# Low parts, evictions, copies and table loads moved within the heads, and the norm factors formed in folded shape at the stage edges

## What is computed

```python
for i in range(DEPTH):
    h = rms_norm(x, W['norm_mix'][i])
    mixed = (hgrn2_mixer, diff_attn_mixer, rwkv7_mixer)[i % 3](h, ...)
    x = x + mixed
    x = x + swiglu(rms_norm(x, W['norm_ffn'][i]), W['ffn_w_in'][i], W['ffn_w_out'][i])
y = rms_norm(x, W['final_norm'])
```

## Time and profile before

| | |
|---|---|
| median of 3 runs | 3368.26 us (3367.20 to 3368.73) |
| the profiled execution, its own time | 3362.62 us |
| its span in the trace | 3361.0 us |
| PE busy | 3209.1 us (95%) |
| DVE busy | 1832.5 us (55%) |
| ACT busy | 1080.8 us (32%) |
| POOL busy | 131.4 us (4%) |
| mean granted PE clock | 0.985 |

### The profile page before, as it was taken

The page is one execution under the profiler, slowest core; times in us unless marked ns, Lnnn a source line. Parts: engine busy times, 40 slices in busy tenths (PEclk is TensorE's granted clock), DMA queues, the critical chain, the costliest instruction groups (busy, mean ns, idle before and its releaser), DMA issues.

```text
span 3361.0 us, 82189 instructions
## 1 busy us (share of the span) xinstructions
PE 3209.1 (95%) x35272; PEld 3041.2 (90%) x35272; DVE 1832.5 (55%) x3017; ACT 1080.8 (32%) x1754; POOL 131.4 (4%) x247
## 2 busy tenths in 40 slices
PE   8998999999998999997999999899999999899998
PEld 7887899998787999996988888899999888799998
DVE  6666643445655543437367887543344666654343
ACT  3222321223555321222434443332223222332221
POOL 0000000001322000000000000000000000000000
PEclk9999999999999999998999999899999999999999
DMA  3322222223433332221210000222232222223222
GB/s 124 102 83 65 85 89 88 86 98 96 129 119 97 87 95 81 88 93 61 82 34 19 12 20 15 61 88 92 83 97 78 84 89 83 71 83 96 81 91 77
DMA packets 104598, 269.08 MB, mean 80 GB/s; under 512 B 12802, under 2 KB 45954, under 8 KB 104146
## 3 DMA queue, kind: packets, MB, share of 16 engines
q1 hardware_dynamic: 91346, 228.54, 21.8%
q0 software_dynamic: 13056, 37.64, 3.4%
HBM read 247.60 MB, written 18.52 MB: 79 GB/s over the span
## 4 chain that ended last, share of the span: by engine, by line
PE 82%; DVE 9%; ACT 3%; DVEq 3%; issue 2%; DMA 1%; SPq 1%; ACTq 0%; POOLq 0%; POOL 0%
PE ps L573 66%; PE ps L1016 5%; DVE arena_r L1924 1%; PE ps L1008 1%; PE ps L654 1%; PE ps L1112 1%; DVE cell L2241 1%; PE ps L712 1%; DVEq L2070 1%; PE ps L735 1%; DVE h L2238 1%; DMA ring<-in_w_mix 1%; DVE arena L2366 1%; DVEq L2240 0%; DVE arena_r L1930 0%
## 5 line engine op out<-in xcount | busy, mean ns | idle before, releaser
L573 PE MATMUL ps<-arena_r 128*128 128x272 f32 x11136 | 1500.7, 293 | 78.2 <-DVE arena_r L1917 22.8
L573 PEld LDWEIGHTS ps<-arena_r 128*128 128x128 f32 x11136 | 1429.9, 190 | 127.3 <-issue 64.1
L573 PE MATMUL ps<-hb_r,arena_r 128*128 128x272 f32 x8448 | 1059.5, 287 | 0.4 <-DVE hb_r L1917 0.4
L573 PEld LDWEIGHTS ps<-hb_r,arena_r 128*128 128x128 f32 x8448 | 1057.4, 188 | 1.1 <-DVE hb_r L1917 0.8
L1415 ACT ACTIVATE arena_r<-ring 128x1024 fp32r<-128x1024 f32 (+1 forms) x240 | 275.8, 1149 | 910.0 <-PE ps L573 910.0
L1943 DVE TENSOR_TENSOR arena_r<-ring,arena_r 128x1024 fp32r<-128x1024 f32 (+1 forms) x240 | 319.7, 1332 | 143.5 <-ACT arena_r L1415 143.5
L1991 DVE TENSOR_TENSOR arena<-ps,rstd 128x544 f32<-128x544 f32 x88 | 63.7, 724 | 291.6 <-PE ps L573 291.6
L2012 DVE TENSOR_TENSOR x<-x,ps 128x544 f32<-128x544 f32 x64 | 46.2, 722 | 291.8 <-PE ps L573 291.8
L1397 ACT ACTIVATE arena_r<-ring 128x1024 fp32r<-128x1024 f32 x80 | 84.8, 1060 | 137.6 <-PE ps L573 132.6
L1462 ACT ACTIVATE arena_r<-arena 128x544 f32 (+1 forms) x88 | 58.2, 661 | 196.0 <-DVE arena L1996 196.0
L1924 DVE TENSOR_TENSOR arena_r<-ring,arena_r 128x1024 fp32r<-128x1024 f32 x80 | 97.6, 1220 | 34.7 <-ACT arena_r L1397 21.9
(11 more groups left out here) (406 smaller groups left out, 3070.2 us busy)
## 6 DMA issues: line engine op xcount, KB each, us to landing
ring<-in_w_up SPq DMA_DIRECT2D x176, 512.0 KB, 3.5
ring<-in_w_mix SPq DMA_DIRECT2D x112, 512.0 KB, 3.5
ring<-in_w_down SPq DMA_DIRECT2D x64, 704.0 KB, 4.0
arena<-in_hg_s POOLq DMA_DIRECT2D x16, 512.0 KB, 3.8
out_hg_so<-arena POOLq DMA_DIRECT2D x16, 512.0 KB, 2.9
ring<-in_w_hgout SPq DMA_DIRECT2D x16, 512.0 KB, 3.5
arena<-in_cache_k SPq DMA_DIRECT2D x128, 64.0 KB, 1.9
arena<-in_cache_v POOLq DMA_DIRECT2D x128, 64.0 KB, 2.2
```

The costliest lines, as they stand in the source:

```text
L573: mm = pe.matmul(PS[:, 2 * a + hf, 0:HALF], part[:, ws], rhs[:, o:o + HALF], start=start and n == 0, stop=stop and n == 2)
```

## The change

- HGRN, each head: the level-0 keys and query are formed ahead of the forget gate and signalled at once; the low part of the next head's unit 1 goes ahead of level 0 (it was behind it); in the last level the keys are multiplied before the queries; the addition of the head's squares goes ahead of the eviction of unit 3.
- HGRN, last head and outputs: the low part of the last output goes ahead of the state update; the second norm is summed in two halves by PE, the last head's squares without DVE; the wait for `st_free` goes behind the outputs. The norm's sums use another PSUM pair, so PE waits for the root ahead of output 2 instead of 3.
- Attention: the wait for the constants' table goes behind the first head's evictions; SP loads unit k of head 1 ahead of the first cached keys; in each head the copy of the last probabilities goes ahead of the sample's exponentials, and behind these a root of one column is taken, which brings the root's table.
- RWKV: its norm takes the folded shape of the final one; ACT squares the last chunk of x first and splits unit 0 behind the square of the chunk before; unit 1 is split after the root; PE multiplies unit 1 one chunk behind unit 0; in each pair from the second on a root of one column is taken ahead of the copy of hv.

The diff, cut to its core:

```diff
@@ attention_units (SP)
                 sp.wait_ge(S("norm_rms"), nth(norm_name(layer, "m")) + 1)
+                load(1, 0, 4)
                 cached_keys(0)
...
+                second_head_on(1, 1)
+                with sp.Fori(2, HEADS - 1) as h:
+                    second_head_on(h, 0)
@@ tensor
+            def norm_part(squares, a, first):
+                for hf in range(2):
+                    mm = pe.matmul(PS[:, 2 * a + hf, 0:HALF], const("ones"), squares[:, hf * HALF:(hf + 1) * HALF],
+                                   start=first, stop=not first, skip_group_check=True)
+                return mm
+            def folded(name):
+                for last in range(2):
+                    if last:
+                        pe.wait_ge(S("norm_sq"), KC * nth(name) + KC)
+                    else:
+                        pe.wait_ge(S("norm_acc"), sums(name) + KC - 2)
+                    src = nm_sq[(KC - 1) % 2] if last else nm_acc
+                    for q in range(4):
+                        mm = pe.matmul(PS[q * 32:(q + 1) * 32, 0, 0:NT // 4], const("ones")[:, 0:32],
+                                       src[:, q * (NT // 4):(q + 1) * (NT // 4)], start=not last, stop=bool(last), skip_group_check=True)
+                mm.then_inc(S("norm_ssq"), 1)
+                pe.wait_ge(S("fin_r"), nth_plain(name) + 1)
+                for q in range(4):
+                    rows = slice(q * 32, (q + 1) * 32)
+                    mm = pe.matmul(PS[:, 4 + q, 0:NT // 4], const("ones")[rows, :], rstd[rows, 0:NT // 4], start=True, stop=True)
+                mm.then_inc(S("fin_mm"), 1)
@@ hgrn (tensor)
+                pe.wait_ge(S("norm_acc"), sums(name_o) + KC - 1)
+                pe.wait_ge(S(L + "out"), HEADS * (j + 1) + 1)
+                norm_part(nm_acc, 2, True)
                 out_block(0, KC - 1)
+                pe.wait_ge(S("norm_sq"), KC * nth(name_o) + KC)
+                norm_part(nm_sq[0], 2, False).then_inc(S("norm_ssq"), 1)
                 out_block(1, KC - 1)
-                pe.wait_ge(S(L + "state"), HEADS * (j + 1) + 1)
-                norm(norm_name(layer, "o"), 3)
                 for m in range(2, KC):
+                    if m == 2:
+                        pe.wait_ge(S("norm_rms"), nth(name_o) + 1)
                     if m == 3:
-                        pe.wait_ge(S("norm_rms"), nth(norm_name(layer, "o")) + 1)
+                        pe.wait_ge(S(L + "state"), HEADS * (j + 1) + 1)
@@ rwkv (tensor)
-                norm(norm_name(layer, "m"), 0)
+                folded(norm_name(layer, "m"))
...
                 for c in range(KC):
                     unit_block(0, c)
-                    unit_block(1, c)
+                    if c:
+                        unit_block(1, c - 1)
+                unit_block(1, KC - 1)
@@ scalar
+            def folded_root(name):
+                act.wait_ge(S("norm_ssq"), nth(name) + 1)
+                act.activation(rstd[:, 0:NT // 4], PS[:, 0, 0:NT // 4], ACT.Sqrt, scale=1024.0 / D, bias=scratch[:, 1:2])\
+                   .then_inc(S("norm_rms"), 1)
@@ after_feed_forward (scalar)
-                if layer + 1 == LAYER_RW and c >= KC - 2:
-                    rw_split(layer + 1, c - (KC - 2))
                 square(norm_name(layer + 1, "m") if layer + 1 < depth else "nfin", x3, c)
+                if layer + 1 == LAYER_RW and c == KC - 2:
+                    rw_split(layer + 1, 0)
@@ attention, mix (scalar)
+                    turned(3)
                     act.wait_ge(S("at_smaxed"), h + 1)
...
                     last.then_inc(S("at_sprobs"), 1)
-                    turned(3)
+                    act.activation(c_table, c_sub, ACT.Sqrt)
@@ rwkv (scalar)
-                root(norm_name(layer, "m"), 0)
+                folded_root(norm_name(layer, "m"))
+                rw_split(layer, 1)
@@ rwkv, pair (scalar)
                     level(h, 5)
+                    if former:
+                        act.activation(c_table, c_gn, ACT.Sqrt)
@@ vector
+            def folded_factor(name):
+                dve.wait_ge(S("norm_rms"), nth(name) + 1)
+                dve.reciprocal(rstd[:, 0:NT // 4], rstd[:, 0:NT // 4]).then_inc(S("fin_r"), 1)
+            def normed_chunk(gain, c):
+                h, x = (ap[:, c, :].rearrange("p (q t) -> p q t", q=4) for ap in (h3, x3))
+                dve.scalar_tensor_tensor(h, x, vec3[:, gain, c:c + 1], PS[:, 4:8, 0:NT // 4], ALU.mult, ALU.mult)\
+                   .then_inc(S("norm_h"), 1)
@@ hgrn, mix (vector)
-                    dve.tensor_scalar(hg_f, hg_sgp, scratch[:, 1:2], scratch[:, 3:4], ALU.mult, ALU.add)
                     dve.tensor_scalar(hg_ks[:, 0:NT], hg_sgn, scratch[:, 1:2], None, ALU.mult)
-                    dve.tensor_tensor(hg_q, hg_qs, hg_qr, ALU.mult)
+                    dve.tensor_tensor(hg_q, hg_qs, hg_qr, ALU.mult).then_inc(S(L + "lvl"), 1)
+                    dve.tensor_scalar(hg_f, hg_sgp, scratch[:, 1:2], scratch[:, 3:4], ALU.mult, ALU.add)
                     dve.drain()
-                    dve.tensor_scalar(hg_f, hg_f, F_MIN, None, ALU.max).then_inc(S(L + "lvl"), 1)
+                    dve.tensor_scalar(hg_f, hg_f, F_MIN, None, ALU.max)
...
+                    hg_rest(layer, h + 1, 1)
                     dprev, doff = hg_f, 0
                     for n in range(LEVELS):
...
+                            if n < LEVELS - 1:
+                                queries()
                             dve.tensor_tensor(kv[:, :, 0, :], kv[:, :, 0, :],
                                               dv[:, :, 1:2].to_broadcast([P, m, blk]), ALU.mult).then_inc(S(L + "lvl"), 1)
+                            if n == LEVELS - 1:
+                                queries()
...
-                        if n == 0 or more and n in (3, 6):
+                        if more and n in (3, 6):
                             hg_rest(layer, h + 1, 1 + n // 3)
...
+                    if not more:
+                        low(L, 2 * KC * j + KC, V_HG + j, o3, hh, hl, KC - 1)
                     for b in range(NB):
...
                     if more:
                         hg_rest(layer, h + 1, 4)
+                        dve.wait_ge(S("norm_sq"), h + (KC * nth(name_o) - j * HEADS + 1))
+                        dve.tensor_tensor(nm_acc, nm_acc, nm_sq[0], ALU.add).then_inc(S("norm_acc"), 1)
                         evict(h + 1, 3)
-                    else:
-                        low(L, 2 * KC * j + KC, V_HG + j, o3, hh, hl, KC - 1)
-                    dve.wait_ge(S("norm_sq"), h + (KC * nth(name_o) - j * HEADS + 1))
-                    dve.tensor_tensor(nm_acc, nm_acc, nm_sq[0], ALU.add).then_inc(S("norm_acc"), 1)
...
-                dve.wait_ge(S(L + "st_free"), HEADS * (j + 1) + 1)
                 for m in range(KC):
...
+                dve.wait_ge(S(L + "st_free"), HEADS * (j + 1) + 1)
@@ attention (vector)
-                dve.wait_ge(S("at_c_in"), 16)
-                signs = at_const("signs")
-                dve.scalar_tensor_tensor(c_sign, signs[:, 1:2], c_nlam, signs[:, 0:1], ALU.mult, ALU.add)
                 factor(norm_name(layer, "m"))
...
                 key_evict(0, True)
                 query_evict(0)
+                dve.wait_ge(S("at_c_in"), 16)
+                signs = at_const("signs")
+                dve.scalar_tensor_tensor(c_sign, signs[:, 1:2], c_nlam, signs[:, 0:1], ALU.mult, ALU.add)
@@ rwkv (vector)
-                factor(norm_name(layer, "m"))
+                folded_factor(norm_name(layer, "m"))
+                rw_rest(layer, 1)
...
+                dve.wait_ge(S("fin_mm"), nth_plain(norm_name(layer, "m")) + 1)
                 normed_input(0)
```

67 lines of the change are left out of this document (25 added, 42 removed).

## The result

The kernel after takes **3317.26 us** (median of 4 runs, 3315.59 to 3318.93) where the kernel before took 3367.73 beside it (4 runs, 3366.88 to 3368.73): a ratio of 0.985, 95% interval 0.9833 to 0.9867. A second comparison (four runs of after, 13 of before) gave 3316.68 against 3363.4: 0.9866 (0.9849 to 0.9882).

The account below looks back on a forecast made before the run. With TensorE busy 3209 of 3361 us, only its 152 us of standing still and low-clock stretches could shrink. Terms 12.2 + 1.6 + 4.4 + 8.1 + 7.6 + 5.1 + 0 = 39.0 took 3368.3 to 3329.3; range 3320 to 3343.

Parts of the forecast that it names:

- the kept distance: Whole kernel: the median of runs was taken to stay 5.6 us above the profiled execution, giving 3329.3 instead of 3323.6.
- Sum 0.54 + 0.33 = 0.87 a trip: HGRN heads: PE's waits for low part and keys shrink by this much, 12.2 us over 14 trips.
- 0.47 + 0.51 = 0.98: Attention heads: us saved in each of seven trips by the earlier copy and root; 7.6 us in all.
- With the place of the median uncertain by 1 to 2 us: Whole kernel: this margin on the median widened the forecast's own 3322 to 3340 to the range 3320 to 3343.
- it gains 0.4 from where the sum went and 0.4 from drains: Last HGRN head: DVE's chain to output 0's low part shortens by 0.8 us each, 1.6 for two.
- The edge into attention: Attention start: PE waits 1.4 us instead of 5.5, clock stays high, second score comes 8.1 us sooner.
- the edge into RWKV: RWKV start: first normalised chunk comes 5.5 us after the last addition instead of 10.6, gaining 5.1.
- the RWKV heads as neutral: RWKV heads: a new 0.6 us wait before the variance offsets the 0.58 gone before the bonus; net 0.0.
- (A): Rival, attention and RWKV heads: the moved table load costs more than 1.3 us; gain 28, time 3340; chance 0.07.
- (B): Rival: the loops give nothing as other DVE or ACT steps replace the waits; gain 19.2, time 3349; chance 0.07.
- (C): Rival, 14 heads: the table preload does not hold and loads are added; gain gone, time 3365; chance 0.03.
- (D): Rival, 29 loop heads: rearranged waits bring a clock drop into each, losing 78 us; time 3407; chance 0.03.

Follow-up runs that it names:

- Low_ahead: Kernel before with only the low part of the next head's unit 1 moved ahead of level 0 in HGRN heads: 3352.63 us, ratio 0.9962.
- copy_first: Kernel before with only ACT's copy of the last probabilities put ahead of the sample's exponentials in attention: 3359.26 us, ratio 0.9978.
- root_ahead: Kernel before with only a one-column square root behind the sample's exponentials in attention, loading the root's table early: 3357.41 us, ratio 0.997.
- keys_first: Kernel before with only the keys made ahead of the queries in the last level of HGRN heads: 3358.52 us, ratio 0.9978.

## Why the prediction was wrong

Its direction and most of its mechanisms held; the forecast of 3329.3 was 12.0 us too high. Of these, 5.6 are the kept distance, 1.7 that after's median lies below its own profiled execution, and 4.6 the terms of the sum, two kinds of them, in opposite directions.

**The price of a stop was mis-sized.** The steps "Sum 0.54 + 0.33 = 0.87 a trip" and "0.47 + 0.51 = 0.98" took the listed idle time as the gain. Low_ahead gave 0.82 for a listed 0.54, copy_first 0.77 for 0.47, root_ahead 0.83 for 0.69 at its place. A stop of PE between blocks cost the listed time, 0.16 for the overlap of matmuls that the row counts as busy (0.28 less 0.125), and in low_ahead 0.11 more behind it. In 14 HGRN trips this is 3.9 us. In attention the trips gave 1.46 instead of 0.98; about half of that lies in the wait of 0.20 in front of L876, which I had not entered since it has another cause, but which the earlier root took along. My bounds were sums of the same listed waits, so both terms came out above their upper ends (16.1 for 13.3, 10.4 for 9). For the keys 0.33 was right (0.34): there a gap of 0.08 stays, as forecast.

**The kept distance was no property of the kernel.** The step "I keep that distance" added 5.6 us. Two profiled executions of one program differ by 3.0 (before) and 5.6 (after), the timed ones of before by 15. Without it the forecast would have been 3323.6, inside the range and still 6 too high. The step "With the place of the median uncertain by 1 to 2 us" failed with it: the three runs in the first table, all within 1.5 us, had made the median look firmer than it is, and later medians of before were 3366.3, 3365.8 and 3363.4, up to 4.9 lower. How much of the distance between 3318.93 and the forecast's 3323.6 is the edit cannot be told to the microsecond either: low clock and loop speed differ between the two executions by chance.

**Terms too large.** The last HGRN head gave 0.5, not 1.6. The step "it gains 0.4 from where the sum went and 0.4 from drains" failed: PE waits 2.07 and then 2.97 there, and the low part of 1.21 between the levels takes what was freed ahead. A term of -3.2 I could not have had: the feed-forward's first loops of layers 0 and 3 ran slower in the execution of after that I compared. In both output edges the reciprocal came as forecast (2.5 and 2.1 for 2.4 and 2.0), but the named wait alone was a fifth of it. The 1.8 from the clock are no merit of the edit: the stretch at the lower clock behind the edge is missing in layer 3 of this execution (38.99 us from the reciprocal to the feed-forward's first block), and the second execution of after has it in both layers (40.45 there).

**What was right.** The edge into attention to the tenth (8.1, the second score 4.47 after the values at clock 1.00, and the key loads did not get in the way); the edge into RWKV (first chunk at 5.27, forecast 5.5), both read from the trace of after; the RWKV heads as neutral (a new wait of 0.44 listed, forecast 0.6; the 0.58 gone; 49.38 for 49.49). Of the rivals, (A) falls: the root starts 0.02 after the end of a load of 1.28 (812.73, 1870.33), and with the root behind the square the load starts 0.01 after the step ahead of it (1868.68). The Trainium skill ("ScalarE: Activation LUTs", section "What ACT_TABLE_LOAD costs") counts a drain of some 1380 ns with every switch of sets; it is not seen in any of these rows. Its 1283 ns for the load agree with the 1.28. (B) falls with low_ahead and keys_first, (C) since the program has 58 loads in either kernel and the real root none in front. (D) did not happen. The trips of the HGRN and attention loops hold no low stretch in any execution (first and last heads do, in both kernels), and those of RWKV come and go with no edit. But the reason that I gave, "in the loops, whose waits are 0.7 at most, no such stretch is seen", was a misreading: the trace of before has three in its RWKV pairs (at 1726, 1774 and 1826 us).

**Left open.** The edge into RWKV and the edits of the last HGRN head were not run alone. Why the first loop of the feed-forward runs at 124.4 ns a matmul in one execution and at 126.1 in the next was not tried. It is no property of the change: both kernels show both.

## What to carry to other kernels

Price a stop of PE from start to start of its neighbours, not by the idle time in brackets: here three of the four stops taken apart were worth 0.1 to 0.3 us more than listed, which in 14 HGRN trips was 3.9 us. A table load belongs behind the last piece of ACT work that PE waits for, in ACT's own idle time; in front of such work it only moves the wait (49.38 to 48.87 a pair). An edit whose halves feed two waits in a row has to be priced whole: half of the attention edge gave nothing, and the most visible wait of the HGRN edge gave a fifth.

## What the runs showed of the hardware that I had not expected

One program, run again, takes another course: matmuls of a loop with PE wholly busy and clock 1.00 stand 124.4 or 126.1 ns apart for 100 us at a time, and stretches of 3.4 us at 0.50 fall into RWKV pairs or not, at 1.54 us for each pair. Together the span of after was 3317.4 once and 3311.8 once, and 67 timed executions of before lay between 3358 and 3374. With four to ten runs a side, the intervals of the comparisons here are 3 to 6 us either way, so a smaller difference needs the trace.
